# Nine weight places in the expert stage, overflow weights by halves, and a reordered routing chain

## The reference

```python
g_logits = t @ w_rg + b_rg                     # 4 groups
e_logits = (t @ w_re + b_re).reshape(N, 4, 8)  # 8 experts in each group
g_sel = argmax(g_logits); e_prob = softmax(e_logits[rows, g_sel])
top_p, top_i = lax.top_k(e_prob, 2)
gates = g_p[:, None] * top_p / sum(top_p)
# for every (token, expert) pair that was chosen:
hid = jax.nn.silu(xb @ w_gate[e]) * (xb @ w_up[e])   # 1024 -> 256
y   = hid @ w_down[e]                                # 256 -> 1024
out = segment_sum(y * gate)                          # two rows for each token
```

## Time and profile before

| | us |
|---|---|
| median of 3 runs | 2986.21 (2985.51 to 2987.89) |
| profiled execution | 2986.71 |
| its span, first to last instruction | 2985.0 |
| TensorE busy | 2913.9 (98%) |
| GpSimd busy | 922.8 (31%) |
| VectorE busy | 1364.1 (46%) |

### The profile page before, as it was taken

One profiled execution on the slowest core, in us unless ns is written; L12 is line 12 of the kernel. 1 busy time (PEld: TensorE's weight loads), 2 busy tenths in 40 slices (PEclk: granted clock), 3 DMA queues, 4 the chain that ended last, 5 costly groups with the idle time before them and its releaser, 6 DMA issues.

```text
span 2985.0 us, 31524 instructions
## 1 busy us (share of the span) xinstructions
PE 2913.9 (98%) x12296; PEld 1856.9 (62%) x12296; DVE 1364.1 (46%) x2249; ACT 609.1 (20%) x1039; POOL 922.8 (31%) x729
## 2 busy tenths in 40 slices
PE   9999999999999999999999999999999999999998
PEld 7865464333468754643333588888664445888887
DVE  6733543333436435432444554442574464644442
ACT  2035323000210263230001400001212351300000
POOL 5500031554124110225551154443220102254442
PEclk9999999999999999999999999999999999999999
DMA  5211125999612201249998222222221111222220
GB/s 192 85 71 43 43 92 186 391 388 393 249 71 87 83 29 57 71 155 370 375 379 328 85 85 85 85 95 88 97 80 57 62 52 57 82 88 85 85 99 29
DMA packets 84165, 412.72 MB, mean 138 GB/s; under 512 B 27572, under 2 KB 30048, under 8 KB 37552
## 3 DMA queue, kind: packets, MB, share of 16 engines
q1 hardware_dynamic: 57664, 387.57, 34.2%
q0 software_dynamic: 26352, 23.12, 2.4%
HBM read 513.31 MB, written 31.46 MB: 183 GB/s over the span
## 4 chain that ended last, share of the span: by engine, by line
PE 89%; DVE 4%; DMA 4%; issue 1%; ACT 1%; SPq 0%; POOL 0%; DVEq 0%; ACTq 0%; POOLq 0%
PE PS L1139 38%; PE PS L1071 9%; PE PS L631 8%; PE PS L1093 5%; PE PS L616 4%; PE PS L709 4%; PE PS L589 4%; PE PS L1312 4%; DMA ring<-in_experts_gu 3%; PE PS L864 1%; PE PS L548 1%; PE PS L804 1%; PE PS L921 1%; PE PS L930 1%; PE PS L1379 1%
## 5 line engine op out<-in xcount | busy, mean ns | idle before, releaser
L3167 POOL TENSOR_TENSOR ATT<-ring 128x512 f32<-128x512 f32 (+1 forms) x97 | 126.3, 1302 | 1178.9 <-PE PS L1139 624.6
L1139 PE MATMUL PS<-G,ATT 128*128 128x256 f32 x1344 | 317.8, 379 | 0.0
L1139 PE MATMUL PS<-HT,ring 128*128 128x256 f32 x1376 | 313.8, 379 | 0.8 <-DVE BIG L1541 0.8
L1139 PE MATMUL PS<-G,ring 128*128 128x256 f32 x1216 | 287.6, 379 | 0.0
L1139 PEld LDWEIGHTS PS<-HT,ring 128*128 128x128 f32 x1376 | 261.2, 190 | 39.5 <-issue 2.4
L1139 PEld LDWEIGHTS PS<-G,ATT 128*128 128x128 f32 x1344 | 255.4, 190 | 36.0 <-issue 1.2
L631 PE MATMUL PS<-HT,ring 128*128 128x512 f32 x576 | 263.3, 600 | 0.0
L1139 PEld LDWEIGHTS PS<-G,ring 128*128 128x128 f32 x1216 | 231.0, 190 | 31.4
L2880 ACT ACTIVATE TMP<-PS 128x256 f32<-128x256 f32 x91 | 35.0, 384 | 1049.0 <-PE PS L1139 931.8
L1071 PE MATMUL PS<-ring,G 128*64 128x512 f32 x1024 | 228.8, 596 | 9.5 <-DMA ring<-in_experts_gu 9.0
L631 PEld LDWEIGHTS PS<-HT,ring 128*128 128x128 f32 x576 | 104.5, 190 | 127.4 <-issue 120.9
(11 more groups left out here) (387 smaller groups left out, 4315.2 us busy)
## 6 DMA issues: line engine op xcount, KB each, us to landing
ring<-in_stream SPq DMA_DIRECT2D x163, 1024.0 KB, 4.8
ring<-in_experts_gu SPq DMA_DIRECT2D x128, 1024.0 KB, 9.8
ring<-in_experts_down SPq DMA_DIRECT2D x64, 1024.0 KB, 8.8
G<-expert_rows SPq DMA_DIRECT2D x8, 1024.0 KB, 7.5
h_tokens<-G POOLq DMA_DIRECT2D x2, 2048.0 KB, 7.6
G<-h_tokens,ATT POOLq DMA_INDIRECT x156, 7.0
XT<-in_xT SPq DMA_DIRECT2D x1, 1024.0 KB, 8.3
G<-in_pT POOLq DMA_DIRECT2D x2, 512.0 KB, 6.4
```

The lines of the kernel that those rows point to most:

```text
L1139: mm = pe.matmul(product(g, name), x[:, k * P:(k + 1) * P], y[:, k, :], start=first and k == 0 and name in opening, stop=last and k == h - ...
L3167: pool.tensor_tensor(a["S1"], a["A21"], a["A22"], ALU.add)\
```

## The change

It has three parts.

1. The expert stage uses nine weight places (`PLACES`): the six of the ring, two in the upper third of `BIG` and one in `ATT` (slots 7 to 10; other users of those slots move to 9, 10, 11 and 12). `Ring.experts` gives the order. SyncE fills the two places in `BIG` when the branches are done, and the one in `ATT` when the output projection is done.
2. Tail weights get a place of 2 MB for each side instead of 3. Gate/up weights come in two transfers by halves (rows of 8 KB) into places that alternate from tail to tail (`tail_place`); the down weights go where the first half lay, and so are issued only after that half was used. Rows of the index `widx` triple. The zeroing of the tail places is gone; the memset of `TMPF` goes to GpSimd.
3. Routing: `logits` goes ahead of all `token_rows`, and all `layer_tile` behind `ranks`; on VectorE the gate values go right before their use, and `widx` behind the index and the table; the token rows are stored in two transfers of 1 MB; ScalarE loads its Silu table right after the Exp.

```diff
+PLACES = 9
+            def experts(self):
+                order = [(self.place + i) % RING if i < RING else i for i in range(PLACES)]
+                for n in range(6 * PAIRS):
+                    p = order[n % PLACES]
+                    self.fills[p] += 1
+                    yield p, self.fills[p]
...
-        TW = BIGF[:, 0:12 * D].rearrange("p (s n) -> p s n", s=2)
+        TW = BIGF[:, 0:8 * D].rearrange("p (s n) -> p s n", s=2)
+        PLACE = ([ring[:, i, :] for i in range(RING)] + [BIGF[:, (16 + 4 * i) * S:(20 + 4 * i) * S] for i in range(2)]
+                 + [ATT[:, 7 * S:11 * S]])
+        def tail_place(n, side, j):
+            i = (n + j) % 2
+            return TW[:, side, i * UNIT:(i + 1) * UNIT]
...
-                token_rows(0)
                 logits()
-                token_rows(1)
-                layer_tile(0)
-                token_rows(2)
-                layer_tile(1)
-                token_rows(3)
+                for t in range(TT):
+                    token_rows(t)
                 ranks()
-                for m in range(2, KD):
+                for m in range(KD):
...
-                        if j == 0:
-                            pe.wait_ge(Q["tail_gu_landed"], now.next("tail_gu_landed", 32))
-                        if j == 2:
-                            pe.wait_ge(Q["tail_down_landed"], now.next("tail_down_landed", 32))
-                        return [TW[:, side, j * UNIT:(j + 1) * UNIT] for side in range(2)], []
+                        landed = ("tail_gu_landed0", "tail_gu_landed1", "tail_down_landed")[j]
+                        pe.wait_ge(Q[landed], now.next(landed, 32))
+                        return [tail_place(ORDER[q][1], side, j) for side in range(2)], []
...
-                pool.memset(BIGF[:, 8 * S:], 0.0).then_inc(Q["tails_zeroed"], now.inc("tails_zeroed"))
-                pool.wait_ge(Q["lin_free"], at[f"htok{L}"])
-                pool.dma_start(HDR.rearrange("(t p) d -> p t d", p=P), HTOK).then_inc(Q["h_stored"], 16)
+                pool.wait_ge(Q["tile_done"], 2 * (at[f"out{L}"][1] + 3))
+                pool.memset(TMPF, 0.0).then_inc(Q["rows_zeroed"], now.inc("rows_zeroed"))
+                for t in range(0, TT, 2):
+                    pool.wait_ge(Q["lin_free"], at[f"htok{L}"] - 2 * (TT - 2 - t))
+                    pool.dma_start(HDR.rearrange("(t p) d -> p t d", p=P)[:, t:t + 2, :], HTOK[:, t:t + 2, :])\
+                        .then_inc(Q["h_stored"], 16)
...
                 gather(0)
                 gather(1)
-                pool.wait_ge(Q["tails_zeroed"], L + 1)
-                pool.wait_ge(Q["rx_zeroed"], 3 * (L + 1))
-                tail_gate_up(L, 0)
-                tail_down(L, 0)
+                pool.wait_ge(Q["widx_ready"], now.next("widx_ready"))
+                pool.wait_ge(Q["rows_zeroed"], L + 1)
+                tail_gate_up(L, 0, 0)
+                tail_gate_up(L, 0, 1)
                 no_rows()
...
-                    if 1 <= q < NSEQ and ORDER[q - 1][0] == "tail" and ORDER[q - 1][1] + 1 < TAILS:
-                        pool.wait_ge(Q["gu_ready"], 2 * (L * NSEQ + q))
-                        tail_gate_up(L, ORDER[q - 1][1] + 1)
+                    if 1 <= q < NSEQ and ORDER[q - 1][0] == "tail":
+                        pool.wait_ge(Q["gu_ready"], 2 * (L * NSEQ + q) - 1)
+                        tail_down(L, ORDER[q - 1][1])
                     if q >= 2:
                         pool.wait_ge(Q["y_ready"], y0 + q - 1)
                         scatter(q - 2)
-                        kind, n = ORDER[q - 2]
-                        if kind == "tail" and n + 1 < TAILS:
-                            tail_down(L, n + 1)
+                    if 1 <= q < NSEQ and ORDER[q - 1][0] == "tail" and ORDER[q - 1][1] + 1 < TAILS:
+                        pool.wait_ge(Q["gu_ready"], 2 * (L * NSEQ + q))
+                        tail_gate_up(L, ORDER[q - 1][1] + 1, 0)
+                    if q >= 2 and ORDER[q - 2][0] == "tail" and ORDER[q - 2][1] + 1 < TAILS:
+                        pool.wait_ge(Q["dn_ready"], L * NSEQ + q - 1)
+                        tail_gate_up(L, ORDER[q - 2][1] + 1, 1)
...
+                sp.wait_ge(Q["lin_ready"], at[f"branches{L}"])
+                weights(RING)
+                weights(RING + 1)
+                for n in range(RING - 1):
+                    weights(n)
+                sp.wait_ge(Q["unit_done"], at[f"out{L}_end"])
+                sp.wait_ge(Q["lin_ready"], at[f"projected{L}"])
+                weights(RING + 2)
+                weights(RING - 1)
+                for n in range(PLACES, len(units)):
+                    weights(n)
```

More of the change, by code:

```diff
@@ L292, in __init__ @@
             def __init__(self):
-                self.place, self.fills = 0, [0] * RING
+                self.place, self.fills = 0, [0] * PLACES
             def next(self):
@@ L1103, in moe @@
                 at[f"moe{L}_y"] = now.count("y_ready")
+                places = plan.experts()
                 turn_x(0)
@@ L1119, in moe @@
                 down(NSEQ - 1)
+                assert next(places, None) is None
                 pe.wait_ge(Q["y_ready"], now.next("y_ready"))
@@ L1301, in _ @@
                 branch(DAQ)
+                at[f"branches{L}"] = now.count("lin_ready")
                 output_projection(f"out{L}", HT, lambda: router(L, 0, 6))
+                at[f"projected{L}"] = now.count("lin_ready")
                 moe(L)
@@ L1974, in moe @@
                     .then_inc(Q["dve_step"], now.inc("dve_step"))
+                v.wait_ge(Q["table_landed"], now.next("table_landed"))
+                v.wait_ge(*now.prev())
+                v.tensor_reduce(r["gsum"], v3(r["ge"][:, 0:16], TT), AX, ALU.add)\
+                    .then_inc(Q["dve_step"], now.inc("dve_step"))
+                v.wait_ge(*now.prev())
+                v.tensor_scalar(r["s4"], r["ge"][:, 16:20], 1.0, None, ALU.add)\
+                    .then_inc(Q["dve_step"], now.inc("dve_step"))
+                v.wait_ge(*now.prev())
+                v.tensor_tensor(r["gsum"], r["gsum"], r["s4"], ALU.mult).then_inc(Q["dve_step"], now.inc("dve_step"))
+                gate = r["gate"].rearrange("p (t c) -> p t c", c=2)
+                v.wait_ge(*now.prev())
+                v.reciprocal(gate[:, :, 0], r["gsum"]).then_inc(Q["dve_step"], now.inc("dve_step"))
+                v.wait_ge(*now.prev())
+                v.tensor_tensor(gate[:, :, 1], gate[:, :, 0], r["ge"][:, 16:20], ALU.mult)\
+                    .then_inc(Q["dve_step"], now.inc("dve_step"))
                 v.wait_ge(*now.prev())
@@ L2836, in moe @@
                 act.activation(r[:, 0:20], r[:, 0:20], ACT.Exp).then_inc(Q["table_landed"], now.inc("table_landed"))
[L2837 to L2842 removed]
+                act.preload_act_table_set("silu_and_others")
+                for m in range(KD):
                     take(HT[:, m, :], None)
@@ L3307, in experts, with weights @@
                     steps += [(q, 0), (q, 1)] + ([(q - 1, 2)] if q else [])
-                for q, j in steps + [(NSEQ - 1, 2)]:
-                    kind, m = ORDER[q]
-                    if kind == "main":
-                        for side in range(2):
-                            e = 2 * m + side
-                            load(A["experts_gu"][L, e, :, j, :] if j < 2 else A["experts_down"][L, e, :, :])
+                units = [(2 * ORDER[q][1] + side, j) for q, j in steps + [(NSEQ - 1, 2)] if ORDER[q][0] == "main"
+                         for side in range(2)]
+                places = list(plan.experts())
+                def weights(n):
+                    place, fill = places[n]
+                    if fill > 1:
+                        name, value = used[(place, fill - 1)]
+                        sp.wait_ge(Q[name], value)
+                    e, j = units[n]
+                    sp.dma_start(PLACE[place], A["experts_gu"][L, e, :, j, :] if j < 2 else A["experts_down"][L, e, :, :])\
+                        .then_inc(w_landed[place], 16)
+                sp.wait_ge(Q["lin_ready"], at[f"branches{L}"])
[9 more added lines that the diff above has]
+                    weights(n)
             for L in range(LAYERS):
```

103 lines of the change are left out of this document (44 added, 59 removed).

## The result

The changed kernel takes **3000.97 us** (median of 7 runs, 2993.24 to 3005.23), the kernel before beside it 2986.99 (7 runs, 2985.51 to 2988.58): ratio 1.0045, interval 1.0035 to 1.0055. It is slower, by 13 to 14 us. The forecast was 2983.4 in a range of 2962 to 3000, so the time is just above the range, where rival B had put it.

The account below looks back on a forecast made before the run. TensorE, 98% busy, could win only its 71 us idle, mostly waits for a full weight supply. 2986.71 - 7.4 routing - 27.3 supply + 30.4 overflow + 1.5 clock = 2983.9; median 0.5 lower, 2983.4; 8-in-10 range 2962 to 3000.

Parts of the forecast that it names:

- rival B: Expert stage: deeper places keep more loads outstanding, landings grow to 10.2 us, kernel slower at 3001 us; chance 0.2.
- the mechanism of the down weights: Overflow blocks: down weights, issued behind four gathers, land after TensorE wants them; waits of 30.4 us in all.
- What bounds the kernel: TensorE is 98% busy at full clock; 27.3 us of its expert-stage waits come from a full weight supply.
- Part 1, routing: Chain from logits to first gather: table read and first turn 3.7 us earlier per layer, 7.4 for two.
- Part 2, nine places: Expert stage: three more places load earlier; 17.8 of 27.3 us saved by supply alone, all if other waits give it time.
- The price of 2.97 us a unit: Weight supply in the expert stage: each 1 MB unit takes 2.97 us, so three places give 8.9 us per layer.
- rival A: Overflow transfers land in time and supply alone decides: 2961.5 us, down to 2952; chance 0.2.
- Part 3, overflow weights: Down weights of overflow blocks arrive late: eight waits of 2.0 us and two of 7.1, 30.4 in all.
- The forecast's own sign of being wrong: Down weights of overflow blocks: the forecast is wrong if their second transfer's landing isn't 7.8 to 9.4 us.
- The sum that I made for the down slot: Second down transfer of an overflow block: 6.7 us of room, landing 8.6, so a wait of 2.0 us.
- my upper bound of 11: Upper end for the landing of overflow down weights, 11 us, at which their waits would sum to 54 us.
- Part 4, clock: TensorE's clock falls only after the two 7 us waits, 0 to 1.5 us each; 1.5 taken for both.

Follow-up runs that it names:

- the second half moved: Changed kernel with only the second gate/up halves of overflow blocks ordered ahead of the scatter: 2996.86 us, ratio 1.0032 to the kernel before.
- the second trace: Second profile of the changed kernel, nothing altered: 3.4 us longer than its first, clock loss 17.0 us; median of that measurement 2999.39 us.
- the better order: Changed kernel, nine places, with down weights ordered ahead of the gathers and second gate/up halves ahead of the scatter: 2974.93 us, ratio 0.9958.

## Why the forecast was wrong, point by point

In short: the mechanism of the down weights was right, and three terms of the sum were mis-sized: clock 7.7 us for 1.5, overflow waits 35.0 for 30.4, routing -4.1 for -7.4. The step that failed in the mechanism is the one that gave the next gate/up halves no cost: they cause 18.8 us of the 35.0.

**What bounds the kernel: half right.** The waits of the earlier trace rows were supply waits, and they vanished. "A weight supply that is full" was read from a share of 1.00. With one more place the share is 1.02 and the rate 405 GB/s in the same window, so a share of 1.00 doesn't show that bytes can't go faster. A clock "full in every slice" was read too far as well: a digit 9 says 90% or more.

**Part 1, routing: mis-sized, -4.1 for -7.4.** The index read came 3.0 and 2.7 us earlier, the first turn 2.46 and 1.65. Layer 0, TensorE's timeline, beside 487.25 in the earlier trace rows:

```profile
484.79 2.03 PE L1051 MATMUL PS<-MATS,G 128*128 128x128 f32 x16 [0.69 <-ACT HT L2842]
```

The first turn used to wait for the gather; it now waits 0.69 us for ScalarE's take of the last layer tile, a wait that the gather had covered. The layer tiles began at 468.33 instead of the 467.8 of the forecast, behind the matmuls that turn the token rows, 7.19 us from 460.27. The granted clock from 459.0 to 466.5 us is 0.54 now and was 0.77 before; that this is what made them late is likely but not shown. In layer 1 the logits were read only 0.7 us earlier (1296.95 for 1297.98, less the 0.32 by which the whole layer starts earlier), and the ranks wait for VectorE's mask:

```profile
1303.12 0.49 PE L1016 MATMUL PS<-ATT,MATS 128*128 128x128 f32 x2 [0.96 <-DVE ATT L1902]
```

I had worked out layer 0 and doubled it. The store in two transfers cost nothing, as forecast.

**Part 2, nine places: the mechanism right, the worth wrong.** That overflow waits take the place of supply waits is right (six places take the same time as nine). The price of 2.97 us a unit was wrong: the first place more is worth 8.5 us a layer, half of the 17.1. It didn't enter the forecast's sum, in which the 27.3 us went whole, but it is in rival A.

**Part 3, overflow weights: the failed step.** Behind the sine tables the mechanism and the size of the down waits hold: the second transfers at 1454.20 and 1531.94 were wanted after 4.0 and 1.8 us and landed after 9.0, for a forecast of 8.6; the waits are 5.2 and 7.3, for 7.1 each. The forecast's own sign of being wrong, a landing of this slot outside 7.8 to 9.4 us, didn't come. In the steady periods, where I had 16.2 us of them, they are in time only because of what I had left out (with the second half moved they are late there too). The forecast said of the next gate/up halves that "their users come a block or more later" and gave them no cost. GpSimd's timeline shows it:

```profile
573.78 1.00 POOL L3158 DMA_INDIRECT BIG<-in_experts_down,ATT  x1 [0.30 <-issue]
575.09 1.00 POOL L3158 DMA_INDIRECT BIG<-in_experts_down,ATT  x1 [0.30 <-issue]
...
589.32 1.03 POOL L3135 DMA_INDIRECT expert_rows<-G,ATT  x1 [1.93 <-DVE G L2085]
590.65 1.03 POOL L3149 DMA_INDIRECT BIG<-in_experts_gu,ATT  x1 [0.30 <-issue]
591.99 0.99 POOL L3149 DMA_INDIRECT BIG<-in_experts_gu,ATT  x1 [0.31 <-issue]
```

The second half for T' goes where T's down weights lay, is issued behind T's scatter, at 591.99, and is wanted at 604.67 - 2.71 = 601.96: 9.97 us of room for a landing of 12.5. The sum that I made for the down slot (room 6.7 for 8.6) wasn't made for this one. With my landing of 8.6 it would still have shown no wait, and with my upper bound of 11 one of 1.2 us; the second halves that TensorE waited for took 11.4 to 13.0, the down weights 8.8 to 9.0. So the missing price has two parts, a sum not made and a landing not foreseen, and why these land later is open. Both waits in one period cover each other, so the total is only 35.0 for my 30.4, which is luck: 18.8 of it is of a kind that I had at nothing. Each of the two, left alone, gives 33.

**Part 4, clock: mis-sized, 7.7 for 1.5.** I costed waits up to 2.4 us at nothing because before none brought it down. There a period's 2.7 us were split into 1.26 and 1.44; now they stand in one piece. That this is why they pay is my reading, not shown: some waits of 2 to 3 us paid and some didn't. Both long waits paid too: the 16 matmuls behind them took 5.12 and 5.50 us for 3.65, which is the upper bound of 1.5 each and a little more.

**The sum again**: -4.1 (routing), -27.3 + 35.0 = +7.7 (waits), +7.7 (clock): +11.3. The trace has +9.2; the rest is VectorE's waits, 5.2 us instead of 7.5. Of the 17.6 us between forecast and result 6 lie in the clock, 5 in the overflow waits and 3 in routing, less 2 for VectorE; the last 5 are that the profiled execution is 5.1 us below the median of its runs, at a clock of 0.995, which by the second trace is clock as well. Rival B had its sign and its time (3001) right, by luck, not its reason: landings of down weights didn't grow to 10.2, and with six places the time and the landings are the same. Rival A, 2961.5 and down to 2952, is what the nine places can do if nothing waits for overflow weights: 2952.4, measured without the transfers; with them and in the better order it is 2974.93. Two small sums of the forecast are off and change nothing: the time for a landing of 6.8 us comes to 2965, and A with a quarter of the forecast to a chance of 0.31.

## What to carry to other kernels

When a load is split so that it can only be issued later, work out room and landing for *every* part against its own user, and move the issue ahead of gathers and scatters before spending memory on depth; look for late transfers that cover each other, since mending one of them shows little. A supply at a DMA share of 1.00 may still gain from one more place, so measure one place, not three. Gaps of 2 to 3 us in TensorE's stream may have to be paid twice: once as waits, once as slower matmuls behind them.

## What was unexpected of the hardware

- An indirect transfer whose indices are all out of range isn't free: each still has 144 packets, and where TensorE waited for one in the changed kernel it landed 8.8 to 13.0 us after its issue. Leaving all of them out brought 48.6 us, waits for them and the slower clock included.
The Trainium skill (DMA: Bandwidth & Descriptors, Anatomy of one DMA) gives a transfer from GpSimd 2.0 us plus its bytes; beside a queue of large loads the runs show more than four times that for next to no bytes written.
- The lower clock came at some single waits of 2 to 3 us and not at others (in one execution at 2.52 us and not at 3.18), and in some executions more often, which goes with run times that spread over 12 us.
- One more place for loads of 1 MB raised the rate of the supply from 385 to 402 GB/s, at a DMA share that was 0.98 before.
